# Value products with the values stationary, in two column groups, in a hybrid attention layer on one core

## The reference

```python
h = rmsnorm(x) * (1 + scale(c)) + shift(c)            # c @ w_ada gives shift, scale, gate
u = h @ w_in                                          # one projection, 2776 columns
q_a, kv_a, g_logit, z_a, cq, ckv, kr, z_b = split(u)
# group A (8 heads of 64 in 2 key/value groups), three branches with gates of their own:
o_cmp = softmax(q . kc + bias) . vc                   # compressed keys, blocks of 32, step 16
o_sel = softmax(q . gathered(ks) + bias) . gathered(vs)   # 16 of the blocks of 64 tokens
o_win = softmax(q . k_win + bias, last 512) . v_win   # local branch
# group B (4 heads), latent keys and values of 128 with a rotary part of 64:
o_lat = softmax((q_lat . ckv + q_rope . k_rope) * s) . ckv
x + gate * (concat[(g0*o_cmp + g1*o_sel + g2*o_win) * silu(z_a), (o_lat @ w_uv) * silu(z_b)] @ w_out)
```

## Time and profile before

| | us |
|---|---|
| median of 3 runs | 1238.36 |
| the profiled execution | 1239.3 |
| its span, first to last instruction | 1237.5 |
| TensorE busy (PE) | 1155.0, 93% |
| VectorE (DVE) | 546.6, 44% |
| ScalarE (ACT) | 315.1, 25% |
| GpSimd (POOL) | 86.9, 7% |

### The profile page before, as it was taken

The page is one execution under the profiler, slowest core; times in us unless marked ns, Lnnn a source line. Parts: engine busy times, 40 slices in busy tenths (PEclk is TensorE's granted clock), DMA queues, the critical chain, the costliest instruction groups (busy, mean ns, idle before and its releaser), DMA issues.

```text
span 1237.5 us, 20840 instructions
## 1 busy us (share of the span) xinstructions
PE 1155.0 (93%) x7894; PEld 776.4 (63%) x7894; DVE 546.6 (44%) x1421; ACT 315.1 (25%) x636; POOL 86.9 (7%) x209
## 2 busy tenths in 40 slices
PE   6785999999999999999899999999999799999997
PEld 2463767644445467878778786865444466666665
DVE  0210111011111247776656555642333477777774
ACT  1111121110111147555434343431111122222220
POOL 0000000000000011111010000000000200000000
PEclk8887999999999999999999999999999899999997
DMA  9524511200000414000000000001882287666660
GB/s 350 217 103 171 120 44 60 87 5 6 4 7 3 72 37 124 1 2 2 1 2 2 1 2 1 2 1 60 174 281 75 81 279 269 226 223 223 220 192 19
DMA packets 83258, 115.94 MB, mean 94 GB/s; under 512 B 30065, under 2 KB 52004, under 8 KB 82136
## 3 DMA queue, kind: packets, MB, share of 16 engines
q1 hardware_dynamic: 83160, 114.61, 29.3%
HBM read 102.31 MB, written 12.27 MB: 93 GB/s over the span
## 4 chain that ended last, share of the span: by engine, by line
PE 77%; issue 9%; DVE 5%; DMA 5%; SPq 2%; ACT 2%; POOL 1%; POOLq 0%; ACTq 0%; DVEq 0%
PE PS L516 13%; PE PS L1332 11%; PE PS L1610 9%; PE PS L1363 7%; PE PS L1313 6%; PE PS L461 5%; DMA AR<-in_x_prompt 4%; PE PS L493 3%; PE PS L1302 3%; PE PS L2001 3%; PE PS L1966 2%; PE PS L2014 2%; PE PS L1309 2%; PE PS L482 1%; DVE AR L2174 1%
## 5 line engine op out<-in xcount | busy, mean ns | idle before, releaser
L1332 PE MATMUL PS<-AR 128*128 128x65 f32 (+1 forms) x1344 | 173.3, 269 | 0.4 <-DVE AR L1503 0.4
L1332 PEld LDWEIGHTS PS<-AR 128*128 128x128 f32 x1344 | 165.0, 192 | 0.6 <-issue 0.6
L516 PE MATMUL PS<-AR 128*128 128x512 f32 (+1 forms) x384 | 161.3, 580 | 2.7 <-DVE AR L768 2.7
L516 PEld LDWEIGHTS PS<-AR 128*128 128x128 f32 x384 | 72.9, 192 | 86.0 <-issue 82.3
L1383 ACT ACTIVATE AR<-PS,SM_ 128x64 f32<-128x64 f32 (+8 forms) x224 | 119.4, 595 | 26.4 <-DVE SM_ L1444 18.6
L1363 PE MATMUL PS<-CA,AR 128*128 128x128 f32 x704 | 116.1, 280 | 0.2 <-ACT AR L1383 0.2
L1610 PE MATMUL PS<-AR 128*128 128x512 f32 x256 | 111.7, 592 | 0.0
L1420 DVE TENSOR_REDUCE SM_<-PS 128x2 f32<-128x512 f32 (+6 forms) x62 | 58.9, 950 | 107.2 <-PE PS L1313 55.2
L1393 ACT ACTIVATE AR<-PS 128x512 f32<-128x512 f32 (+1 forms) x108 | 59.1, 547 | 175.5 <-PE PS L1363 175.1
L1363 PEld LDWEIGHTS PS<-CA,AR 128*128 128x128 f32 x704 | 80.6, 148 | 30.3 <-issue 20.5
L1610 PEld LDWEIGHTS PS<-AR 128*128 128x128 f32 x256 | 47.8, 190 | 56.0 <-issue 56.0
(11 more groups left out here) (337 smaller groups left out, 1352.1 us busy)
## 6 DMA issues: line engine op xcount, KB each, us to landing
AR<-in_cache_nsa SPq DMA_DIRECT2D x128, 256.0 KB, 5.1
AR<-in_cache_mla SPq DMA_DIRECT2D x128, 96.0 KB, 4.3
AR<-in_x_prompt SPq DMA_DIRECT2D x16, 512.0 KB, 5.2
AR<-in_w_ada SPq DMA_DIRECT2D x3, 2048.0 KB, 12.1
AR<-in_w_in SPq DMA_DIRECT2D x1, 5888.0 KB, 19.6
out<-AR SPq DMA_DIRECT2D x9, 512.0 KB, 3.0
AR<-in_w_ada SPq DMA_DIRECT2D x8, 512.0 KB, 3.9
AR<-in_w_out SPq DMA_DIRECT2D x4, 1024.0 KB, 9.7
```

Of the source, the lines that this page charges most:

```text
L516: mm = pe.matmul(PS[0:n, bank, 0:hi - lo], ht(j, k)[:, 0:n], w2cols(k, lo, hi), start=(k == 0), stop=(k == KT - 1))
L1332: mm = pe.matmul(out, tile, v, start=(n == 0), stop=(n == nb - 1))
```

## The change

The values of the selected and local branch become stationary (64 columns), and the turned probabilities move (128 columns). The two heads of a unit have different value groups; group 0 writes PSUM partitions 0 to 63, group 1 partitions 64 to 127, and tiles of the two heads take turns. So a group's output comes out with head dimensions on partitions. At the end of a group ScalarE copies it to SBUF (`out_copy`, 256 columns, into `OT`), TensorE turns it back (`back`, two transposes) into columns 256 to 511 of the same bank, and then VectorE finishes. The sums, which came from the column of ones, now come from the exponentials' `accum_out` into `TOT`. Chunks of these branches go in pairs on TensorE: turn two, then the values of two. All finishes stand one chunk later. cmp and mla keep their value products.

In the projection, x of tile j + 3 is loaded at step j (before: j + 2 at step j, from step 1 on), behind the wait for the transposes of tile j + 1; the ada rows of step j + 1 are loaded behind the same count of `s_gk` as before, one step later in the list; W2 comes in four pieces at steps 1 to 4; VectorE scales tile 1 after the modulation. GP is loaded after attention, behind the first x, as `OT` uses its place. Two semaphores become one (`s_gs` goes into `s_gsb`, with counts 16 higher), and TensorE waits for 64 on `s_w2`, not 16. The same bytes are loaded.

```diff
@@ -199,6 +199,7 @@
 TB = [view(49568 + 256 * n, 256) for n in range(2)]
+OT = [view(o, 256) for o in (46496, 46752)]
@@ -253,6 +254,7 @@
 RCB, CFB = ([small(4) for _ in range(2)] for _ in range(2))
+TOT = [small(4) for _ in range(4)]
@@ -350,9 +352,9 @@
     for j in IDX:
-        if 1 <= j <= 6:
-            sp.wait_ge(s_xt, j + 1)
-            sp.dma_start(xs(j + 2), x_t[j + 2]).then_inc(s_x[(j + 2) % 3], 16)
+        if j + 3 <= 8:
+            sp.wait_ge(s_xt, j + 2)
+            sp.dma_start(xs(j + 3), x_t[j + 3]).then_inc(s_x[(j + 3) % 3], 16)
@@ -363,12 +365,11 @@
                 .then_inc(s_cst, 16)
-        if j + 2 < KT:
-            sp.wait_ge(s_gk, 2 * j + 2)
-            sp.dma_start(ADAG[j % 2], ada_v[:, j + 2, 2048:3072]).then_inc(s_adag[j % 2], 16)
-        if j == 1:
-            sp.wait_ge(s_mod, 4)
-            sp.dma_start(W2[:, :, :], w_in2[:, :, W1N:W1N + W2N]).then_inc(s_w2, 16)
+        if 2 <= j + 1 < KT:
+            sp.wait_ge(s_gk, 2 * j)
+            sp.dma_start(ADAG[(j + 1) % 2], ada_v[:, j + 1, 2048:3072]).then_inc(s_adag[(j + 1) % 2], 16)
+        if 1 <= j <= 4:
+            sp.dma_start(W2[:, 2 * j - 2:2 * j, :], w_in2[:, 2 * j - 2:2 * j, W1N:W1N + W2N]).then_inc(s_w2, 16)
@@ -676,8 +677,7 @@
     dve.tensor_copy(GQT, PS[:, 0, 136:138]).then_inc(s_ctv, 1)
-    for j in range(2):
-        dve_scale(dve, j)
+    dve_scale(dve, 0)
@@ -692,6 +692,7 @@
     ins.then_inc(s_modt, 1)
+    dve_scale(dve, 1)
@@ -1221,7 +1222,14 @@
 AV_LAG = 2
-FIN_AT = {c: [og for og, g in enumerate(GROUPS) if CH_OF[g[3]][-1] + AV_LAG + 1 == c] for c in range(NCH + 3)}
+TURNS_BACK = [kind in ("sel", "win") for kind, i, half, last in GROUPS]
+OUT_AT = {c: [og for og, g in enumerate(GROUPS) if TURNS_BACK[og] and CH_OF[g[3]][-1] + AV_LAG + 1 == c]
+          for c in range(NCH + 4)}
+FIN_AT = {c: [og for og, g in enumerate(GROUPS) if CH_OF[g[3]][-1] + AV_LAG + 2 == c] for c in range(NCH + 4)}
+
+def crossed(u):
+
+    return UNITS[u][0] in ("sel", "win")
@@ -1239,13 +1247,15 @@
         return probs(u, 2 * t, 0, P)
-    return probs(u, t // nb, P * (t % nb), P * (t % nb) + P)
+    gi, n = (t % 2, t // 2) if crossed(u) else (t // nb, t % nb)
+    return probs(u, gi, P * n, P * n + P)
 def exps_for(c):
     u, t0, nt = CHUNKS[c]
-    per = 1 if UNITS[u][0] == "cmp" else UNITS[u][5]
-    return EX0[u] + (len(UNITS[u][3]) if UNITS[u][0] == "cmp" else (t0 + nt - 1) // per + 1)
+    if UNITS[u][0] == "mla":
+        return EX0[u] + (t0 + nt - 1) // UNITS[u][5] + 1
+    return EX0[u] + len(UNITS[u][3])
@@ -1254,12 +1264,13 @@
             nb = UNITS[v][5]
-            first = len(PSLOTS[v]) == 2 and PSLOTS[v][0] == PSLOTS[u][n]
+            first = len(PSLOTS[v]) == 2 and PSLOTS[v][0] == PSLOTS[u][n] and not crossed(v)
             need = max(need, (CH_OF[v][(nb - 1) // 4] if first else CH_OF[v][-1]) + 1)
     return need
 s_qk, s_mx, s_neg, s_exp, s_trc = (sem(f"s_at_{n}") for n in ("qk", "mx", "neg", "exp", "trc"))
 s_evA, s_evD, s_av, s_fin = (sem(f"s_at_{n}") for n in ("evA", "evD", "av", "fin"))
+s_ot, s_bt = sem("s_at_ot"), sem("s_at_bt")
@@ -1322,13 +1333,14 @@
             continue
-        (r, g), n = heads[t // nb], t % nb
+        (r, g), n = (heads[t % 2], t // 2) if crossed(u) else (heads[t // nb], t % nb)
         kb = key_tiles(kind, i, k0, nb)[n]
         if kind == "mla":
             out, v = ob[:, 129 * (r % 2):129 * (r % 2) + 129], VM[:, kb, r, :]
         else:
-            slot = 2 * (r % 2) + g
-            out, v = ob[:, 65 * slot:65 * slot + 65], (VS1 if kind == "sel" else VW1)[:, kb, g, :]
+            mm = pe.matmul(ob[64 * g:64 * g + 64, P * (r % 2):P * (r % 2) + P],
+                           (VS1 if kind == "sel" else VW1)[:, kb, g, 0:64], tile, start=(n == 0), stop=(n == nb - 1))
+            continue
@@ -1344,6 +1356,21 @@
         pe_values(pe, c)
+
+    def turns(u, c):
+        _, t0, nt = CHUNKS[c]
+        pe.wait_ge(s_exp, exps_for(c))
+        if c >= 2:
+            wait_copied(pe, c - 2)
+        for t in range(t0, t0 + nt):
+            mm = pe.transpose(PS[:, 4 + c % 2, P * (t - t0):P * (t - t0) + P], tile(u, t), ident)
+        mm.then_inc(s_trc, 1)
+
+    def back(og):
+        pe.wait_ge(s_ot, sum(TURNS_BACK[:og + 1]))
+        for n in range(2):
+            mm = pe.transpose(PS[:, 6 + og % 2, 256 + P * n:256 + P * n + P], OT[og % 2][:, P * n:P * n + P], ident)
+        mm.then_inc(s_bt, 1)
@@ -1354,19 +1381,21 @@
             pe_scores(pe, v).then_inc(s_qk, 1)
-        for c in CH_OF[u]:
-            _, t0, nt = CHUNKS[c]
-            pe.wait_ge(s_exp, exps_for(c))
-            if c >= 2:
-                wait_copied(pe, c - 2)
-            for t in range(t0, t0 + nt):
-                mm = pe.transpose(PS[:, 4 + c % 2, P * (t - t0):P * (t - t0) + P],
-                                  tile(u, t), ident)
-            mm.then_inc(s_trc, 1)
-            if c >= AV_LAG:
-                values(c - AV_LAG)
-    for c in range(NCH - AV_LAG, NCH):
-        values(c)
+        step = 2 if crossed(u) else 1
+        for c0 in CH_OF[u][::step]:
+            pair = [c for c in CH_OF[u] if c0 <= c < c0 + step]
+            for c in pair:
+                turns(u, c)
+            for c in pair:
+                if c >= AV_LAG:
+                    values(c - AV_LAG)
+                for og in OUT_AT[c]:
+                    back(og)
+    for c in range(NCH, NCH + AV_LAG + 2):
+        if c < NCH + AV_LAG:
+            values(c - AV_LAG)
+        for og in OUT_AT[c]:
+            back(og)
@@ -1380,8 +1409,19 @@
                 act.wait_ge(s_trc, room_for(u, gi))
+            if crossed(u):
+                slot = 2 * (heads[gi][0] % 2) + heads[gi][1]
+                if og >= 4:
+                    act.wait_ge(s_fin, og - 3)
+                act.activation(probs(u, gi, 0, n), PSF[:, o:o + n], ACT.Exp, bias=NM[:, u % 2, gi:gi + 1],
+                               scale=-1.0, accum_out=TOT[og % 4][:, slot:slot + 1]).then_inc(s_exp, 1)
+                continue
             act.activation(probs(u, gi, 0, n), PSF[:, o:o + n], ACT.Exp,
                            bias=NM[:, u % 2, gi:gi + 1], scale=-1.0).then_inc(s_exp, 1)
+
+    def out_copy(og):
+        act.wait_ge(s_av, CH_OF[GROUPS[og][3]][-1] + 1)
+        act.activation(OT[og % 2], PS[:, 6 + og % 2, 0:256], ACT.Copy).then_inc(s_ot, 1)
@@ -1389,10 +1429,15 @@
         for c in CH_OF[u]:
+            for og in OUT_AT[c]:
+                out_copy(og)
             if BY_A[c]:
                 evac(act, c, lambda o, i: act.activation(o, i, ACT.Copy), s_evA)
         if u + 1 < N and not early(u + 1):
             expo(u + 1)
+    for c in range(NCH, NCH + AV_LAG + 2):
+        for og in OUT_AT[c]:
+            out_copy(og)
@@ -1456,14 +1501,17 @@
                 evac(dve, c, dve.tensor_copy, s_evD)
-    for c in range(NCH, NCH + AV_LAG + 1):
+    for c in range(NCH, NCH + AV_LAG + 2):
         for og in FIN_AT[c]:
             dve_finish(dve, og)
 def dve_finish(dve, og):
     kind, i, half, last = GROUPS[og]
-    dve.wait_ge(s_av, CH_OF[last][-1] + 1)
+    if TURNS_BACK[og]:
+        dve.wait_ge(s_bt, sum(TURNS_BACK[:og + 1]))
+    else:
+        dve.wait_ge(s_av, CH_OF[last][-1] + 1)
@@ -1478,13 +1526,14 @@
         return
-    o = ob[:, 0:260].rearrange("p (h c) -> p h c", h=4)
+    o = ob[:, 0:260].rearrange("p (h c) -> p h c", h=4) if kind == "cmp" else \
+        ob[:, 256:512].rearrange("p (h c) -> p h c", h=4)
     if kind == "cmp" and i == 0:
         dve.tensor_scalar(RC, o[:, :, 64], 1e-30, None, ALU.max).then_inc(s_cl, 1)
         dve.wait_ge(s_cl, half + 1)
         dve.reciprocal(RC, RC).then_inc(s_rc, 1)
     else:
-        dve.reciprocal(RC, o[:, :, 64]).then_inc(s_rc, 1)
+        dve.reciprocal(RC, o[:, :, 64] if kind == "cmp" else TOT[og % 4]).then_inc(s_rc, 1)
@@ -1545,10 +1594,10 @@
     sp_scratch(sp)
-    sp.dma_start(GP, gate_dram[8:9, :].to_broadcast([P, DM])).then_inc(s_gp, 16)
     sp.wait_ge(s_fin, NG)
     sp.wait_ge(s_pz, 2 * NT)
     sp.dma_start(XO[0], x_t[1]).then_inc(s_xo[0], 16)
+    sp.dma_start(GP, gate_dram[8:9, :].to_broadcast([P, DM])).then_inc(s_gp, 16)
...
```

More of the change, by code:

```diff
@@ L272, in build @@
         s_vs, s_oA, s_kT, s_kTe = sem("s_vs"), sems("s_oA", 2), sem("s_kT"), sem("s_kTe")
-        s_oW, s_gs, s_gsb = sem("s_oW"), sem("s_gs"), sem("s_gsb")
+        s_oW, s_gsb = sem("s_oW"), sem("s_gsb")
         s_cos = sem("s_cos")
@@ L386, in sp_projection @@
                     sp.wait_ge(s_gate, 1)
-                    sp.dma_start(gs_dram, GATS[0:RS, :]).then_inc(s_gs, 16)
+                    sp.dma_start(gs_dram, GATS[0:RS, :]).then_inc(s_gsb, 16)
             sp.wait_ge(s_modD, 2)
@@ L402, in sp_projection @@
                 .then_inc(s_wu, 16)
-            sp.wait_ge(s_gs, 16)
+            sp.wait_ge(s_gsb, 16)
             for h in range(H):
@@ L496, in pe_projection @@
                 pe_keys(pe, j)
-            pe.wait_ge(s_w2, 16)
+            pe.wait_ge(s_w2, 64)
             for j in IDX:
```

(6 more changed lines are left out.)

## The result

| | before | after |
|---|---|---|
| median of the runs, us | 1239.7 (4 runs, 1238.31 to 1242.4) | 1219.08 (4 runs, 1218.13 to 1219.97) |
| profiled execution, its span | 1239.3, 1237.5 | 1219.97, 1218.2 |

What follows compares the result with a forecast made beforehand. TensorE seemed to bound attention, with waits on late loads in the projections. Projections -30.75 and attention -8 (tiles 0 to 3 -7, tiles 4 to 7 -1) summed to -38.75: 1200 us from 1239.3 profiled, range 1184 to 1217.

Steps and rivals of the forecast that it cites:

- Projections, -30.75: Projections: earlier x loads and W2 in pieces remove four waits (25.4 us) and the slow groups behind them; 30.75 us saved.
- Rival D: Projections: x still comes late because other loads and stores share the queue; half of the 31 stays, 1215 us; chance 0.08.
- TensorE's count in attention: Attention: faster value instructions save 58 us, less 24 for 96 returns and 7 for turning back; TensorE's work falls 27.
- Rival C: Value products at L1332: column groups do not run side by side; about 1283 us; chance 0.03 slower, 0.02 about as before.
- Tiles 4 to 7, -1: Attention's far query tiles: loop gains of 8.5 us nearly cancelled by 7.4 for the output copy; 1 us saved.
- The copy ahead of the exponentials: Tiles 4 to 7: ScalarE's output copy delays exponentials, making some units 5.1 us long; +7.4 us in all.
- The loops: Tiles 4 to 7: the cycle scores, minimum, bias, exponentials, next scores sets unit length once TensorE is faster; -8.5 us.
- The -1.8 for local units: Part of the loop sum in tiles 4 to 7: 16 local units, each 0.11 us shorter.
- Rival A: Attention: TensorE's count decides, as the copy comes early and the loop has slack; -30.75 - 27 gives 1180 us; chance 0.13.
- Tiles 0 to 3, -7: Attention's near query tiles stay bound by TensorE, whose shorter units give -8.3 us, counted as -7.
- Waits of VectorE's finish: Attention: finishes one chunk later and behind the turn back cost nothing, as the bank pair is next written a group later.
- Rival B: Attention: new waits of about 0.9 us also cost clock, 12 to 25 us; 1212 to 1225 us; chance 0.14.

Runs made afterwards that it cites:

- e5: e4 with the finishes of cmp and mla back in their old place; 1203.54 us, ratio 0.9708.
- e12: Old attention with the new projections (as e1), plus 12 spare transposes ahead of attention's first unit; 1203.29 us, ratio 0.9704.
- e3: Changed kernel with sum buffers TOT counted by turned groups, so exponentials wait only for the finish of the buffer's last user; 1216.53 us, ratio 0.9785.
- e4: e3 with copy, turn back and finish one chunk later where nb is over 4; 1201.27 us, ratio 0.9704.
- e8: e5 without the exponentials' sums (TOT filled with ones, so no softmax division there); 1202.77 us, ratio 0.9671.
- e1: Kernel before with only the projection's edits (load order, moved scaling of tile 1), attention as before; 1206.7 us, ratio 0.9722.

## Why the prediction was wrong, step by step

**Projections, -30.75: right.** Measured -33.1 between the profiles, -34.8 as a kernel alone. L508 starts 31.4 us earlier; where the other 1.7 come from stays open. All four waits went, the groups behind them are back at 7.21 and 7.03, and W1 takes the start, at no gain. Rival D fell. That GP lies later was not seen as a wait.

**TensorE's count in attention: right for each instruction, not in the sum.** Value instructions 0.054 (0.055 forecast), a return about 0.3 (0.25). Rival C fell: the two column groups run side by side with different moving data (a move of 512 columns without column groups takes 7.03 / 16 = 0.44, so 128 would take 0.11). The sum left a term out. Of the 32 turns back, 16 in e5 stand between values of the same unit; each breaks the run of 64-column values in two and adds a return of its own, so there are 112 returns and not 96. By busy time TensorE's work fell by 15.4 us (370.29 in e12, 354.89 in e5), where 27 was forecast. Small slips beside it: with returns hidden the bound is 58 - 7 = 51, not 45; 172.14 + 128 x 0.055 is 179.18, not 179.13; and the four unit terms of tiles 0 to 3 add up to -8.5, not -8.3.

 The rule of the Trainium skill ("TensorE: Matmul & The Clock Gate", Part 3) that a weight load overlaps only when the row groups differ does not hold in this trace, where 12 products with a weight load each take 0.88 us, 0.054 each.

**Tiles 4 to 7, -1: the copy right, the loops not, off by 3.** The copy ahead of the exponentials, forecast at +7.4, cost about 7.9 from e3 to e4; the local units alternate 4.56 and 5.21 us (4.5 and 5.1 forecast). The loops, forecast at -8.5, gave -4.0 with the copy out of the way (249.5 to 245.5): tiles 4 to 7 changed by -0.1, -0.2, -1.5 and -2.3. The -1.8 for local units is not there; in e5 one takes 4.59, as before (4.61). The loop of 4.38 was read rightly (e8 shows it), but two sums cost it 0.21 and not 0.12. Which of the smaller terms failed beside it was not separated. That the stage lost only 2.3 between the two profiles is also because before had some 3 us of lowered clock in it (252.6 against 249.5 in e12). Rival A fell: TensorE's count does not decide.

**Tiles 0 to 3, -7: the step that failed,** 20.9 us off. "Waits of VectorE's finish, now one chunk later and behind TensorE's turn back, are covered" was said of TensorE's wait for its bank. The same diff adds a second reader of that counter, ScalarE's `act.wait_ge(s_fin, og - 3)` ahead of the exponentials of a group, and the prediction names no such wait. That is the first failure of the step; the second is its count of TensorE's work. Three parts, as far as the stages tell them apart (0.6 is left over):
- 6.4 us: that wait and the clock behind it, in tiles 1 and 2 (27.0 + 36.1 after, 56.7 in e3). Shown by e3, which takes away the wait and gets the clock of 1.00 back. The same wait in tiles 3 and 4 cost nothing.
- 5.1 us in tile 0 (21.2 after, 16.1 in e5), with a clock of 0.68; 1.0 of it went in e3. The fall isn't the new products' alone, e1 has it too. The four runs of the change lie within 1.9 us, so probably all had it; whether its finish waits make the fall surer was not tried.
- 8.8 us: the gain that was never there, since e5 with full clock and no such wait needs 131.7 where 129.9 were needed before. Tiles 1 to 3 changed by +0.5, -0.7 and -1.2 from before to e5, where the prediction's terms for their units give -1.2, -3.0 and -4.9. Waits do not explain it: in e5 TensorE is busy for all of the 32.16 us of tile 2. The turns back do, in part. First before, then e5, in tile 2 (unit starts are the scores, L1313 and L1328; L1376 is the turn back):

```profile
512.26 0.92 PE L1313 MATMUL PS<-AR 64*128 64x384 f32 x4
...
515.15 0.92 PE L1313 MATMUL PS<-AR 64*128 64x384 f32 x4
```
```profile
478.44 0.92 PE L1328 MATMUL PS<-AR 64*128 64x384 f32 x4
...
480.90 0.92 PE L1328 MATMUL PS<-AR 64*128 64x384 f32 x4
481.75 0.88 PE L1370 MATMUL PS<-CA,AR 128*128 128x128 f32 x6
482.55 0.66 PE L1345 MATMUL PS<-AR 128*64 128x128 f32 x8
483.14 0.44 PE L1376 MATMUL PS<-CA,AR 128*128 128x128 f32 x2
483.51 0.44 PE L1345 MATMUL PS<-AR 128*64 128x128 f32 x4
483.88 0.92 PE L1328 MATMUL PS<-AR 64*128 64x384 f32 x4
```

A unit took 2.89 us and takes 2.46, 0.43 less where 0.38 was forecast. But one with a turn back among its values takes 2.98: the turn back costs 0.52, not the 0.22 of two transposes, and the gain of the unit is gone. The rest lies in tile 0 (+1.1) and the run of cmp (+1.9), where TensorE does wait (2.2 and 2.8 us free in e5); ScalarE has 9.4 us more to do in the whole stretch than in e12, but whether that or the copy between values and finish holds these two up was not separated.

**Rival B** (new waits cost clock, 1212 to 1225, given 0.14) has the right mechanism in the wrong place, and the right time in part by luck, since 8.8 us of the miss are a gain that did not come: I put it at the late exponentials of tiles 4 to 7, whose clock stayed at 0.97 to 1.00; it struck behind waits of 2 to 3 us in tiles 1 and 2.
